# A hybrid recurrent trunk layer in float32: turns of two output tiles in one place, level 0 of an inversion turned by a product, another order of the first loads, shorter last row pieces

## The chip, the cores and the metric

The kernel runs on one core of a Trainium2 chip. Its metric is the device time of one execution in microseconds, the median of three runs. The engines that count here are TensorE (PE in the rows; its weight loads are PEld), VectorE (DVE), ScalarE (ACT), GpSimd (POOL) and the sync engine's queue that issues every DMA (SP). Each engine executes its own instructions in order, and waits between engines are semaphores.

## What is computed

One layer over 592 rows of width 2048: 64 rows of a later-chunk request, 16 learned meta rows and 512 rows of a prompt.

```
h = rmsnorm(x, norm_pre);  P = h @ w_in          # 2048 x 15504
A: mLSTM, 8 heads x 128      B: HGRN2, 4 heads x 128      C: RWKV-7, 8 heads x 64
merged = sum_b sigmoid(gate_b(h)) * (y_b @ w_proj_b)
x' = x + rmsnorm(merged @ w_out, norm_post)      # 576 rows are kept

rwkv_step:
    sa = einsum('bhvk,bhk->bhv', s_state, -kk)
    s_new = s_state * w + sa (kk * a)^T + v k^T
    y = einsum('bhvk,bhk->bhv', s_new, r)
```

The outputs are the rows of x' and the states of the three branches. The RWKV branch is done in chunks of up to 128 rows, for which a unit lower triangular matrix has to be inverted per chunk and head.

## The kernel before

**Products.** Every weight tile is a block of 2048 x 128 float32 values. It comes by DMA to `w_raw` (two slots), ScalarE rounds it to `w_hi` (`split_hi`), VectorE takes the rest into `w_lo` (`split_lo`), and `product(n)` (line 990) multiplies it in 16 blocks by the activations, which are kept in the same way as `act_hi` and `act_lo`. One block is three matmuls (hi by hi, lo by hi, hi by lo) per range of columns. `stages` hangs other TensorE work ahead of a given block, so that it runs inside the stream of matmuls.

**Start.** SP issues the loads in the order of lines 725 to 733: the vectors of weights (`vecs`), rows 0 to 127 of x, the constants (`full`, which holds the identity), the other rows of x, two weight tiles, the masks. For each of five row tiles ScalarE squares the rows (line 1698), GpSimd makes 1/rms of the sums in two small operations (lines 3031, 3033), VectorE scales the rows (line 2166), and TensorE turns them. VectorE's loop stands behind `dve.wait_ge(vecs_here, 16)` at line 2161, ScalarE's behind the same wait at line 1691. The first product needs the fifth row tile.

**RWKV.** There are four rounds, each with two heads. The inversion keeps the inverse of the levels done so far in `DD1` and goes up through levels 0 to 6. Level 0 is made by VectorE in `EE0` (lines 2642 to 2644) from a block unit matrix that GpSimd writes (line 3073). TensorE turns `EE0` by ten transposes (`turn_first`, line 1368, which calls `turn_squares`) ahead of block 19, and ScalarE copies the result to `DD1` in five pieces (`squares_out`, line 1948). Level 1 begins ahead of block 22 (`level_a_d(1)`), and its second half stands ahead of block 24 (`level_d_a_d(1)`, L1322 in rows) and waits for VectorE's step `low1`. Between `inv0` and `low1` VectorE has the token shift of v (`mixed`, lines 2153 to 2156), a `split_lo` and the masking of level 1.

**Output.** The last stage multiplies by w_out in two parts p: columns 0 to 319 and then 320 to 575, 16 tiles each. When a tile is done, ScalarE copies it out of PSUM (`evacuate`, line 2112, into `zt[0]` or `zt[1]`), TensorE turns it into rows (`turn_out`, line 1622; three transposes for p = 0, two for p = 1), ScalarE sums the squares of these rows (`square_rows`, line 2120), and VectorE stores the scaled rows in `YT` (`rows_out`, line 2969). The loops of TensorE take tiles 2i+1 and 2i+2 per round, the loops of ScalarE tiles 2i and 2i+1. ScalarE's order in a round is

```
evacuate(2i); split_hi(2i+2); square_rows(i, 0); evacuate(2i+1); split_hi(2i+3); square_rows(i, 1)
```

and `turn_out(p, i, j)` waits for `evacuate(2i+j)`, `square_rows(i, j)` for `turn_out(p, i, j)`. At the end of a round TensorE waits in `rows_taken` for the squares and rows of `j = 1`.

**End.** After the last tile VectorE finishes row tiles 3 and 4 (`finish`, line 2985) in halves of 1024 columns, and SP stores each half behind the count `rows_done`.

## Time and profile before

| what | us |
|---|---|
| median of three runs | 2223.01 |
| lowest and highest | 2221.34, 2223.16 |
| the profiled execution | 2221.52 |
| its span, first to last instruction | 2219.7 |
| TensorE busy in it | 2186.7 |
| VectorE, ScalarE, GpSimd busy | 1347.9, 788.0, 63.8 |

The rows quoted further down are of the profiled execution. "Busy" says that an engine had an instruction in flight. A row of the timeline gives start, length, engine, source line, operation and tiles; matmuls overlap, so that the cost of one is the distance between two starts and not its length. What stands in brackets is the idle time of the engine before it and what ended it.

### The profile page before, as it was taken

How to read it: one execution, taken by the hardware profiler on the slowest of the kernel's cores; microseconds unless marked ns; L12 is line 12 of the kernel's file. 1: busy time of each engine (PE TensorE's matmuls, PEld its weight loads, DVE VectorE, ACT ScalarE, POOL GpSimd, SP SyncE). 2: the span in 40 equal slices, each digit the busy share in tenths (PEclk: the TensorE clock that was granted, in tenths of full speed). 3: DMA queues.
4: the chain of work that ended last, by engine and by line, in shares of the span. 5: the costliest groups of instructions: out<-in, count | busy, mean ns of one | idle time of the engine just before them, and what ended most of it. 6: DMA issues, size and time to landing. Idle time of an engine off the chain costs nothing.

```text
span 2219.7 us, 44655 instructions
## 1 busy us (share of the span) xinstructions
PE 2186.7 (99%) x18901; PEld 2151.0 (97%) x18901; DVE 1347.9 (61%) x2105; ACT 788.0 (36%) x1209; POOL 63.8 (3%) x93
## 2 busy tenths in 40 slices
PE   6999999999999999999999999999999999999997
PEld 5999999999999999999999999999999999999997
DVE  5444444488777777676657484755777755454354
ACT  5321221234333333333334242424333443244443
POOL 0000001000000000000000000000000000000000
PEclk9999999999999999999999999999999999999999
DMA  5422222233333333334112121204111353434465
GB/s 184 134 79 97 84 86 90 76 106 119 121 135 110 120 120 124 126 119 169 59 52 83 42 74 45 88 22 151 67 67 67 112 207 139 163 138 171 151 216 181
DMA packets 67352, 249.33 MB, mean 112 GB/s; under 512 B 9082, under 2 KB 16428, under 8 KB 50612
## 3 DMA queue, kind: packets, MB, share of 16 engines
q1 hardware_dynamic: 67204, 247.14, 32.1%
q8 instruction: 120, 1.97, 0.4%
q14 instruction: 28, 0.23, 0.0%
HBM read 216.92 MB, written 30.19 MB: 111 GB/s over the span
## 4 chain that ended last, share of the span: by engine, by line
PE 98%; DMA 1%; DVE 0%; SPq 0%; ACT 0%; issue 0%; DVEq 0%; POOL 0%; ACTq 0%; POOLq 0%
PE acc L1009 52%; PE acc L1198 16%; PE branch L1198 8%; PE acc L1608 7%; PE branch L1608 2%; PE branch L1297 1%; PE branch L1497 1%; PE branch L1313 1%; PE branch L1322 1%; DMA scratch<-in_x_all 1%; PE acc L1052 1%; PE branch L1287 0%; PE branch L1365 0%; PE branch L1628 0%; PE branch L1144 0%; PE branch L1137 0%
## 5 line engine op out<-in xcount | busy, mean ns | idle before, releaser
L1009 PE MATMUL acc<-act_hi,w_hi 128*128 128x320 f32 (+3 forms) x2848 | 869.0, 305 | 0.0
L1009 PE MATMUL acc<-act_lo,w_hi 128*128 128x320 f32 (+3 forms) x2848 | 845.4, 297 | 0.0
L1009 PE MATMUL acc<-act_hi,w_lo 128*128 128x320 f32 (+3 forms) x2848 | 845.4, 297 | 0.0
L1009 PEld LDWEIGHTS acc<-act_hi,w_hi 128*128 128x128 f32 x2848 | 537.3, 189 | 11.0 <-issue 5.0
L1009 PEld LDWEIGHTS acc<-act_lo,w_hi 128*128 128x128 f32 x2848 | 537.2, 189 | 0.7
L1009 PEld LDWEIGHTS acc<-act_hi,w_lo 128*128 128x128 f32 x2848 | 537.0, 189 | 0.0
L2149 DVE TENSOR_TENSOR w_lo<-w_raw,w_hi 128x2048 fp32r<-128x2048 f32 x119 | 272.5, 2290 | 228.1 <-ACT w_hi L1666 225.6
L1666 ACT ACTIVATE w_hi<-w_raw 128x2048 fp32r<-128x2048 f32 x120 | 229.8, 1915 | 132.9 <-PE branch L1608 125.7
L1198 PE MATMUL acc<-corner_terms,w_hi 128*128 128x288 f32 x768 | 154.5, 296 | 0.0
L1198 PE MATMUL acc<-act_hi,w_hi 128*128 128x288 f32 x512 | 151.6, 296 | 0.0
L1198 PE MATMUL acc<-act_lo,w_hi 128*128 128x288 f32 x512 | 151.4, 296 | 0.0
L1198 PE MATMUL acc<-act_hi,w_lo 128*128 128x288 f32 x512 | 151.0, 295 | 0.0
L1198 PEld LDWEIGHTS acc<-corner_terms,w_hi 128*128 128x128 f32 x768 | 123.1, 188 | 0.0
L1816 ACT ACTIVATE w_hi<-w_raw 128x1024 fp32r<-128x1024 f32 x72 | 76.2, 1060 | 126.3 <-PE acc L1198 82.9
L1608 PE MATMUL acc<-act_lo,w_hi 128*128 128x288 f32 x384 | 113.4, 295 | 0.0
L1816 ACT ACTIVATE w_hi<-scratch 128x1024 fp32r<-128x1024 f32 x72 | 76.2, 1058 | 104.4 <-PE acc L1198 55.8
L1608 PE MATMUL acc<-act_hi,w_hi 128*128 128x288 f32 x384 | 113.2, 295 | 0.0
L1608 PE MATMUL acc<-act_hi,w_lo 128*128 128x288 f32 x384 | 113.1, 294 | 0.0
L1198 PE MATMUL acc<-corner_terms,w_lo 128*128 128x288 f32 x384 | 113.1, 294 | 0.0
L2346 DVE TENSOR_TENSOR w_lo<-w_raw,w_hi 128x1024 fp32r<-128x1024 f32 x72 | 87.8, 1219 | 36.7 <-ACT w_hi L1816 36.7
L1678 ACT ACTIVATE scratch<-acc 128x64 f32<-128x64 f32 (+1 forms) x38 | 8.3, 219 | 254.5 <-PE acc L1009 254.5
L1198 PEld LDWEIGHTS acc<-act_hi,w_lo 128*128 128x128 f32 x512 | 96.5, 188 | 0.0
(470 smaller groups left out, 3502.9 us busy)
## 6 DMA issues: line engine op xcount, KB each, us to landing
w_raw<-in_w_stream SPq DMA_DIRECT2D x122, 1024.0 KB, 4.8
w_raw<-in_w_stream SPq DMA_DIRECT2D x96, 512.0 KB, 5.9
gate_logits<-gate_out SPq DMA_DIRECT2D x48, 288.0 KB, 2.2
scratch<-gate_logits SPq DMA_DIRECT2D x48, 288.0 KB, 5.2
scratch<-in_x_all SPq DMA_DIRECT2D x9, 512.0 KB, 6.0
branch_rows<-branch_out SPq DMA_DIRECT2D x16, 288.0 KB, 2.2
scratch<-in_x_all SPq DMA_DIRECT2D x3, 1024.0 KB, 10.7
out_y_prompt<-scratch SPq DMA_DIRECT2D x6, 512.0 KB, 3.0
```

Of the source, the lines that this page charges most:

```text
L1009: last = mm(acc[s][:, at:at + hi - lo], a[:, s, w], b[:, k, lo:hi], start=(k == order[0] and a is whi and b is xh), stop=(k == order[-1] a ...
L1052: last = mm(acc[0][:, at:at + hi - lo], a[:, 0, P * k:P * k + P], b[:, k, lo:hi], start=(k == 0 and a is whi and b is xh), stop=(k == KT - ...
L1198: last = mm(bank, a[slot][:, w], b[:, k, :], start=(k == 0 and a is q_hi and b is x[0]), stop=(k == KH - 1 and a is q_lo))
L1297: last = mm(bank[:, P * c:P * c + P], lhs[r, span(c)], rhs[r, span(c)], start=True, stop=True)
L1313: last = mm(bra[to, JOIN_AT + 32 * n:JOIN_AT + 32 * n + 32], AT[r, q, r], first, start=True, stop=True)
L1322: last = mm(bra[r, o:o + 32], d, UU[at_, n, 0:32], start=True, stop=True)
L1497: last = mm(brb[r, o + 64 * c:o + 64 * c + 64], k[:, tok], q[:, tok], start=True, stop=True)
L1608: last = mm(banks3[b][:, at:at + hi - lo], x[:, s, w], y[:, k, lo:hi], start=(k == ks[0] and x is whi and y is xh), stop=(k == ks[-1] and ...
L1666: f(whi[:, s, :], wraw[:, s, :], ACT.Copy).then_inc(hi_done, 1)
L1816: R_["hi"].done(f(q_hi[slot], src, ACT.Copy), name)
L2149: v.tensor_tensor(wlo[:, s, :], wraw[:, s, :], whi[:, s, :].bitcast(F32), ALU.subtract).then_inc(lo_done, 1)
L2346: return R.done(v.tensor_tensor(out, a, b, op), step)
```

## The change

There are five edits.

1. The loads are issued as x rows 0 to 127, x rows 128 to 255, `full`, the rest of x, `vecs`, the two weight tiles, the masks. ScalarE's wait for `vecs` moves behind its squares. VectorE's wait for `vecs` stays where it was, ahead of its first scaling (line 2167 now).
2. `full` gets two columns of zeros ahead of the identity, so that `next_row`, the identity moved by one column, can be read from it.
3. RWKV level 0: `turn_first` waits for the step `yk1` and issues one matmul of 320 columns. VectorE subtracts its result from a second block unit matrix, which GpSimd writes into `DD1`. The copy of one block of `EE0`, the ten transposes and ScalarE's five copies are gone. Level 1 waits for VectorE's `turned_inv0`.
4. Output stage: both turns of a round stand ahead of block 3 of product 2i+2; product 2i+1 has none. This holds for seven rounds of each part. ScalarE's and VectorE's order is as before.
5. Row tiles 3 and 4 are finished and stored in pieces of 512, 512, 1024 and 1024, 512, 512 columns.

```diff
-    full = {"ident": np.eye(P), "blocks": s // 64 == t // 64}
+    full = {"lead": np.zeros((P, 2)), "ident": np.eye(P), "blocks": s // 64 == t // 64}
...
+        next_row = full[:, CONST_AT["ident"][0] - 1:CONST_AT["ident"][1] - 1]
...
+        LAST_PIECES = [(3, (0, D // 4)), (3, (D // 4, D // 2)), (3, (D // 2, D)), (4, (0, D // 2)), (4, (D // 2, D // 4 * 3)), (4, (D // 4 * 3, D))]
...
-            sp.dma_start(vecs[:, :], vecs_in).then_inc(vecs_here, 16)
             for t in range(5):
                 for a, b, src in given(t, ROWS[t]):
                     sp.dma_start(xt[a:b, t, :], src).then_inc(x_here[t], 16)
-                if t == 0:
+                if t == 1:
                     sp.dma_start(full[:, :], full_in).then_inc(consts_here, 16)
+            sp.dma_start(vecs[:, :], vecs_in).then_inc(vecs_here, 16)
...
-            for m in range(4):
+            for m in range(len(LAST_PIECES)):
                 sp.wait_ge(rows_done, 4 + m)
-                rows_out(3 + m // 2, m % 2)
+                last_rows_out(m)
...
                     if lv == 1:
-                        pe.wait_ge(*at.after(i, "t0"))
+                        pe.wait_ge(*vt.after(i, "turned_inv0"))
...
                 def turn_first():
-                    pe.wait_ge(*vt.after(i, "inv0"))
-                    turn_squares(EE0, 0)
+                    pe.wait_ge(*vt.after(i, "yk1"))
+                    pt.done(mm(brb[:, 0:320], next_row, UU[:, :, 0:32], start=True, stop=True), "turned0")
...
-                    product(OUT_N + 1, {3: [lambda: turn_out(0, 0, 0)], 4: [lambda: pe.wait_ge(lo_done, OUT_N + 2)]},
-                            unevacuated=KT, cols=cols[0], in_pieces=True)
-                    product(OUT_N + 2, {3: [lambda: turn_out(0, 0, 1)]}, unevacuated=KT, cols=cols[0])
+                    product(OUT_N + 1, {4: [lambda: pe.wait_ge(lo_done, OUT_N + 2)]}, unevacuated=KT, cols=cols[0], in_pieces=True)
+                    product(OUT_N + 2, {3: [lambda: turn_out(0, 0, 0), lambda: turn_out(0, 0, 1)]}, unevacuated=KT, cols=cols[0])
                     rows_taken(0, 0)
                 with looped(pe, 1 - p, top) as i:
-                    product(Num(OUT_N + KT * p, 2, i, 1), {3: [lambda: turn_out(p, i, 0)]}, unevacuated=KT, cols=cols[p])
-                    product(Num(OUT_N + KT * p, 2, i, 2), {3: [lambda: turn_out(p, i, 1)]}, unevacuated=KT, cols=cols[p])
+                    product(Num(OUT_N + KT * p, 2, i, 1), unevacuated=KT, cols=cols[p])
+                    product(Num(OUT_N + KT * p, 2, i, 2), {3: [lambda: turn_out(p, i, 0), lambda: turn_out(p, i, 1)]}, unevacuated=KT, cols=cols[p])
                     rows_taken(p, i)
...
-            act.wait_ge(vecs_here, 16)
             act.wait_ge(*S0["setup_pool"].after(0, "zeros"))
...
+            act.wait_ge(vecs_here, 16)
             act.wait_ge(w_here[0], 16)
...
-                act.wait_ge(*G.after(i, "turned0"))
-                squares_out(lambda r, qs: DD1[r, qs, :], 0)
...
-                tt(EE0[:, 0:10, 1::2], EE0[:, 0:10, 1::2], UU[:, :, 0:32], ALU.subtract, "inv0_part")
-                own("inv0_part")
-                V.done(v.tensor_copy(EE0[64:128, 10, :], EE0[64:128, 0, :]), "inv0")
+                tt(EE0[:, 0:10, 1::2], EE0[:, 0:10, 1::2], UU[:, :, 0:32], ALU.subtract, "inv0")
+                dve.wait_ge(*Q.after(i, "turned_unit_blocks"))
+                dve.wait_ge(*G.after(i, "turned0"))
+                tt(DD1[:, 0:10, 0::2], DD1[:, 0:10, 0::2], brb[:, 0:320].rearrange("p (q n) -> p q n", q=10), ALU.subtract, "turned_inv0")
...
+                Q.done(g.tensor_tensor(DD1[:, 0:10, :], each, each, ALU.mult), "turned_unit_blocks")
                 Q.done(g.memset(DDT[:, :, :], 0.0), "square_zeros")
```

How the instructions stand at the places that matter is shown in three pairs. The first is SP's queue at the start, before.

```order
L725 DMA vecs<-in_vecs_in 128x109
L728 DMA scratch<-in_x_all 64x2048 x2
L730 DMA full<-in_full_in 128x256
L728 DMA scratch<-in_x_all 128x2048 x3
L728 DMA scratch<-in_x_all 64x2048
L728 DMA scratch<-in_x_all 16x2048
L732 DMA w_raw<-in_w_stream 128x2048 x2
```

And the same place of the changed kernel.

```order
L729 DMA scratch<-in_x_all 64x2048 x2
L729 DMA scratch<-in_x_all 128x2048
L731 DMA full<-in_full_in 128x258
L729 DMA scratch<-in_x_all 128x2048 x2
L729 DMA scratch<-in_x_all 64x2048
L729 DMA scratch<-in_x_all 16x2048
L732 DMA vecs<-in_vecs_in 128x109
L734 DMA w_raw<-in_w_stream 128x2048 x2
```

The vectors moved behind all rows of x. VectorE's first row of the changed kernel is still `L2172 TENSOR_SCALAR` with a wait for `vectors_loaded`.

The second place is VectorE at level 0 of the RWKV inversion, before. The first row writes `EE0`, the copy makes its eleventh block, and the row of 593 columns is the first step of v's token shift.

```order
L2522 TENSOR_TENSOR scratch<-scratch 128x320 [waits rwkv_vector]
L2519 REGISTER_ALU
L2644 COPY scratch<-scratch 64x64 [waits rwkv_vector]
L2153 TENSOR_TENSOR scratch<-scratch 128x593 [waits tile_evacuated]
L2154 REGISTER_ALU
L2155 SCALAR_TENSOR_TENSOR scratch<-scratch,head_scalars 128x64 [waits rwkv_vector]
L2156 SCALAR_TENSOR_TENSOR scratch<-scratch,head_scalars 128x528
```

The same place of the changed kernel.

```order
L2528 TENSOR_TENSOR scratch<-scratch 128x320 [waits rwkv_vector]
L2649 REGISTER_ALU
L2650 REGISTER_ALU [waits rwkv_pool]
L2528 TENSOR_TENSOR scratch<-scratch,branch 128x320 [waits rwkv_tensor]
L2159 TENSOR_TENSOR scratch<-scratch 128x593 [waits tile_evacuated]
L2160 REGISTER_ALU
L2161 SCALAR_TENSOR_TENSOR scratch<-scratch,head_scalars 128x64 [waits rwkv_vector]
L2162 SCALAR_TENSOR_TENSOR scratch<-scratch,head_scalars 128x528
```

The copy is replaced by an operation that waits for GpSimd and for TensorE's new matmul, and everything behind it on VectorE stands behind that wait.

The third place is TensorE in the loop of the output stage for p = 0, before. The rows with gate_out are one `turn_out`.

```order
L1009 MATMUL acc<-act_lo,w_hi 128x320
L1009 MATMUL acc<-act_hi,w_lo 128x320
L1625 REGISTER_ALU
L1628 MATMUL branch<-full,gate_out 128x128 [waits tile_evacuated]
L1628 MATMUL branch<-full,gate_out 128x128
L1628 MATMUL branch<-full,gate_out 64x128
L1009 MATMUL acc<-act_hi,w_hi 128x320
L1009 MATMUL acc<-act_lo,w_hi 128x320
```

The same place of the changed kernel, in product 2i+2.

```order
L1018 MATMUL acc<-act_hi,w_lo 128x320
L1637 MATMUL branch<-full,gate_out 128x128 [waits tile_evacuated]
L1637 MATMUL branch<-full,gate_out 128x128
L1637 MATMUL branch<-full,gate_out 64x128
L1634 REGISTER_ALU
L1637 MATMUL branch<-full,gate_out 128x128 [waits tile_evacuated]
L1637 MATMUL branch<-full,gate_out 128x128
L1637 MATMUL branch<-full,gate_out 64x128
L1018 MATMUL acc<-act_hi,w_hi 128x320
```

The second turn, with its own wait for an evacuation, now follows the first without a matmul between them. ScalarE, which serves both waits, has in the changed kernel the order that it had:

```order
L2126 ISA [waits out_tensor]
L2126 ACTIVATE branch_out,mlstm_scalars<-branch 128x128
L2126 ISA
L2126 ACTIVATE branch_out,mlstm_scalars<-branch 128x128
L2126 ISA
L2126 ACTIVATE branch_out,mlstm_scalars<-branch 64x128
L2116 REGISTER_ALU
L2118 ACTIVATE gate_out<-acc 128x320 [waits tile_product_done]
L1674 ACTIVATE w_hi<-w_raw 128x2048 [waits tile_product_done,weights_loaded1]
```

The three squares wait for the first turn (`out_tensor`), and the evacuation of the odd tile (L2118) stands behind them.

## Rows read from the trace of the kernel before

**Rows 1.** The page's busy times: engine, us, share of the span, instructions.

```profile
PE 2186.7 (99%) x18901; PEld 2151.0 (97%) x18901; DVE 1347.9 (61%) x2105; ACT 788.0 (36%) x1209; POOL 63.8 (3%) x93
```

**Rows 2.** Timeline of TensorE, output stage p = 0: start, length, operation.

```profile
2004.52 0.31 PE L1009 MATMUL acc<-act_hi,w_lo 128*128 128x320 f32 x1
2004.67 0.49 PE L1628 MATMUL branch<-full,gate_out 128*128 128x128 f32 x3
...
2005.15 0.31 PE L1009 MATMUL acc<-act_lo,w_hi 128*128 128x320 f32 x1
```

**Rows 3.** Timeline of TensorE, output stage p = 1.

```profile
2185.24 0.29 PE L1009 MATMUL acc<-act_hi,w_lo 128*128 128x256 f32 x1
...
2185.36 0.38 PE L1628 MATMUL branch<-full,gate_out 128*128 128x128 f32 x2
...
2185.70 0.28 PE L1009 MATMUL acc<-act_lo,w_hi 128*128 128x256 f32 x1
```

**Rows 4.** Timeline of ScalarE and VectorE, output stage p = 0.

```profile
2003.52 0.44 ACT L2112 ACTIVATE gate_out<-acc 128x320 f32<-128x320 f32 x1 [2.27 <-PE acc L1009]
...
2005.65 0.27 ACT L2120 ACTIVATE branch_out<-branch 128x128 f32<-128x128 f32 x1
...
2006.31 0.20 ACT L2120 ACTIVATION_READ_ACCUMULATOR branch_out<-branch  x1
...
2005.80 2.29 DVE L2149 TENSOR_TENSOR w_lo<-w_raw,w_hi 128x2048 fp32r<-128x2048 f32 x1 [0.93 <-ACT w_hi L1666]
2008.00 0.42 DVE L2969 TENSOR_TENSOR scratch<-branch,scratch 128x256 f32 x1
```

**Rows 5.** Timeline of the end, all engines.

```profile
2208.06 0.38 ACT L2112 ACTIVATE gate_out<-acc 128x256 f32<-128x256 f32 x1 [3.96 <-PE acc L1009]
...
2208.50 0.44 PE L1628 MATMUL branch<-full,gate_out 128*128 128x128 f32 x2 [0.47 <-ACT gate_out L2112]
...
2209.03 0.28 ACT L2120 ACTIVATE branch_out<-branch 128x128 f32<-128x128 f32 x1 [0.59 <-PE branch L1628]
...
2211.03 4.87 DVE L2985 SCALAR_TENSOR_TENSOR scratch<-scratch,small 128x1024 f32<-128x1024 f32 x4 [0.82 <-DVE scratch L2969]
...
2212.34 3.92 SPq L953 DMA_DIRECT2D out_y_prompt<-scratch  x4
```

**Rows 6.** Timeline of the start, ScalarE and VectorE.

```profile
12.33 1.29 DVE L2166 TENSOR_SCALAR scratch<-scratch,small 128x2048 f32<-128x2048 f32 x1 [12.33 <-POOL small L3033]
...
21.29 1.91 ACT L1698 ACTIVATE scratch<-scratch 80x2048 f32<-80x2048 f32 x1 [1.64 <-DMA scratch<-in_x_all]
...
23.51 0.63 ACT L1700 ACTIVATE w_hi<-w_raw 128x512 fp32r<-128x512 f32 x1 [0.22 <-DMA w_raw<-in_w_stream]
...
24.23 0.42 DVE L2166 TENSOR_SCALAR scratch<-scratch,small 80x384 f32<-80x384 f32 x1 [2.36 <-POOL small L3033]
```

**Rows 7.** Timeline of TensorE, first RWKV round, and one float32 product.

```profile
1060.70 0.66 PE L1266 MATMUL branch<-scratch,full 128*128 128x296 f32 x2
...
1090.02 0.28 PE L1009 MATMUL acc<-act_hi,w_lo 128*128 128x272 f32 x1
1090.23 1.31 PE L1365 MATMUL branch<-full,scratch 128*128 128x128 f32 x10
1091.30 0.40 PE L1009 MATMUL acc<-act_hi,w_hi 128*128 128x320 f32 x1
...
1097.03 1.36 PE L1322 MATMUL branch<-scratch 64*64 64x32 f32 x40
```

**Rows 8.** Timeline of VectorE and GpSimd, first RWKV round.

```profile
1090.21 1.96 DVE L2153 TENSOR_TENSOR scratch<-scratch 128x593 f32<-128x593 f32 x1
...
1095.33 0.49 DVE L2522 TENSOR_TENSOR scratch<-branch,masks 128x320 f32<-128x320 f32 x1
...
1087.76 1.26 POOL L3073 TENSOR_TENSOR scratch<-masks 128x640 f32<-128x640 bf16 x1 [46.96 <-PE branch L1297]
...
1090.08 1.45 POOL L3076 TENSOR_TENSOR corner_terms<-scratch,corner_terms 128x592 fp32r<-128x592 f32 x1
```

19 lines of the change are left out of this document (13 added, 6 removed).

## The prediction

> **What bounds the kernel now.** I read the page's busy times first: TensorE is busy for 2186.7 us of the 2219.7 us span [rows 1]. The rest is the start, where it waits for the first rows of x, and the end, where the last rows are normalised and stored. So an edit is worth what it does to TensorE's own stream, to the time at which that stream starts, or to what follows its last matmul. Busy time saved on VectorE, ScalarE or GpSimd is worth nothing unless TensorE waits for it. Then I read the timeline at the four places the edits touch: both parts of the output stage [rows 2, 3, 4], the end [rows 5], the start [rows 6] and level 0 of the RWKV inversion [rows 7, 8]. At each I ask two things: how long TensorE's own work takes there, and how early the others are with what it waits for next.
>
> The sum is made against the profiled execution, 2221.5 us, which is 1.5 us below the median of 2223.0.
>
> **The output turns.** A place with three transposes costs TensorE 0.33 us: from 2004.52 to 2005.15 are 0.63 us, of which two steps of 0.15 us are matmuls [rows 2]. A place with two costs 0.22 us: 0.46 us less two steps of 0.12 us [rows 3]. The third transpose is therefore worth 0.11 us and two are worth 0.22 us, so no fixed price of a place is left that sharing one could save. I take 0.0 us for it, and 0.1 us a round (twice the 0.05 us that reading two starts can miss) as the most it could give.
>
> What the edit adds is a wait. In the shared place the second turn waits for the evacuation of tile 2i+1. On ScalarE that evacuation stands behind `square_rows(i, 0)`, which waits for the first turn, which is issued just ahead of it in the same place. Before the change the first turn had been done a whole product earlier, and ScalarE was free when tile 2i+1 ended. Now TensorE's queue stands still while ScalarE does the squares and the evacuation, and nothing else is in that queue to fill the time. The price, counted from the start of the first turn, for p = 0:
>
> - the three transposes end after 0.49 us [rows 2];
> - ScalarE starts 0.08 us after the end of a turn (2208.50 + 0.45 to 2209.03) [rows 5], at 0.57;
> - three squares with their sums take 0.86 us (2005.65 to 2006.31 + 0.20) [rows 4], to 1.43;
> - the evacuation of 320 columns takes 0.44 us [rows 4], to 1.87;
> - TensorE starts 0.06 us after the end of an evacuation (2208.06 + 0.38 to 2208.50) [rows 5], at 1.93;
> - the second turn and the way back into the matmuls cost 0.33 us, to 2.26.
>
> Two separate places cost 0.66 us, so a round costs 1.60 us more. For p = 1 the terms are 0.38, 0.08, two squares in 0.61 (0.86 less one step of 0.25), 0.38, 0.06 and 0.22, together 1.73 us against 0.44: 1.29 us more. There are seven such rounds in each part: 7 x 1.60 + 7 x 1.29 = **+20.2 us**. From below the wait can't be shorter than the evacuation and the squares without the two hand-overs (1.46 and 1.15 us, 18 us in all). From above each round may lose another 0.4 us to register work and to starting ScalarE cold: 26 us.
>
> Is anything late next? The odd tile's weights are rounded behind that evacuation. Before, the low part began 2.28 us after the evacuation's start, took 2.29 us, and the row operation after it ended at 2008.42, which is 4.90 us after [rows 4]. TensorE, for p = 1, needs 0.38 + 0.06 + 0.22 us and 13 blocks of three matmuls at 0.12 us [rows 3], 4.68 us, so it comes to the end of the product 5.34 us after the evacuation's start. That leaves some 0.4 us. For p = 0 the product is longer and the margin over 1 us. Only in the first round of p = 1, where VectorE also finishes 128 rows of the first part, do I expect it to be used up; 0.2 us is inside the rounding of the sum.
>
> **The start.** ScalarE and SP no longer wait for the vectors, but VectorE's first scaling does, and the vectors are now queued behind all of x. Before, the scaling of the first row tile began at 12.33 us, and the first 384 columns of the fifth began at 24.23 us [rows 6]; only the fifth was on the path. The last rows of x landed at 21.3 us (ScalarE's square at 21.29 had waited for them) and the first weight tile at 23.5 us [rows 6]. The vectors are queued between the two. The bytes ahead of the vectors' end are the same as those ahead of x's end before, so I take 21.3 us; 23.5 us is the other end. From then VectorE has four scalings of up to 1.29 us [rows 6] to do that were all done before; at 1.25 us each the fifth starts at 26.3 us in place of 24.23: +2.1 us. GpSimd's two small operations for the fifth tile, which lay in the 1.03 us between the square's end (23.20) and 24.23, now fall between VectorE's scalings; I add 0.3 us for that. **+2.4 us**. Everything on TensorE behind it moves by that much, since the fifth tile's turns release the first product. The ends are: nothing at all (the small load overtakes x; even 0.4 us earlier, as x is issued earlier) and +4.3 us (the vectors land with the weights). Issuing x first gains nothing while VectorE waits. The later `full` is hidden, as the first turn is later still.
>
> The Trainium skill (SBUF — State Buffer, Who interferes with whom) says that VectorE's `tensor_scalar` can run in a mode that locks a port shared with GpSimd, and that whoever starts first blocks the other for the whole instruction. By that rule each of GpSimd's two operations could wait for the end of a scaling and hold the next one up by its own length; the 0.3 us would then be up to 0.75 us. No row of the kernel before has the two beside each other at the start.
>
> **Level 0 of the RWKV inversion.** TensorE came to block 19 at about 1090.15 us (0.13 after 1090.02) and was back in its matmuls at 1091.30: 1.15 us, of which ten transposes are 1.07 us [rows 7]. The new matmul has 320 float32 columns; two of 296 columns took 0.66 us, the second of them ending 0.41 us after its start, so one step is 0.25 us [rows 7], and 320 columns are 0.27 us. TensorE saves 1.15 - 0.27 = 0.88 us a round. It is back only if VectorE keeps up, and VectorE now waits for this matmul. The matmul ends at 1090.15 + 0.43, VectorE's subtraction from PSUM takes 0.49 us, as the operation of that size at 1095.33 did [rows 8], and the token shift of v starts at about 1091.14 in place of 1090.21 [rows 8]: 0.93 us later. Before, `low1` was done at 95.33 + 0.49 = 1095.82, and TensorE asked for it at 1097.03 [rows 7, 8], so the reserve was 1.2 us. Now `low1` comes at 1096.75 and TensorE, 0.88 us earlier, asks at 1096.15. It waits 0.6 us, and 0.23 us a round are left. Four rounds: **-0.8 us** (I round down what is left, since GpSimd is busy longer too). ScalarE's five copies were never waited for.
>
> The step of 593 columns at 1090.21 took 1.96 us, though the operation of 320 columns took 0.49 us, and GpSimd's operation of 592 columns lay over it, from 1090.08 to 1091.53 [rows 8]. So about 1.1 us of it were a wait for GpSimd. GpSimd gets one more operation of 1.26 us [rows 8], so its operation of 592 columns starts at about 1091.3, just behind VectorE's step. If VectorE gets through first and isn't held up later, it wins 1.1 us, TensorE doesn't wait, and the gain is 4 x 0.88 = 3.5 us. If it is held up in the next step for all of 1.45 us, 0.25 us more are lost and the gain is 0. I take the middle, the same hold-up as before.
>
> The same section of the Trainium skill says that a VectorE operation with two SBUF inputs contends with a GpSimd operation that reads SBUF, and that the order of issue decides who blocks. The row agrees with the first half. By the second VectorE's step would pass, GpSimd would take the port when it ends, and VectorE's next step would be held up in its place; the sum of this part would then be 0 to -0.8 us.
>
> **The end.** VectorE finishes the last rows in four pieces in 4.87 us, SP issues their stores from 2212.34 on, and the span ends at 2219.7 [rows 5]. With a first piece of half the size the first store starts some 0.55 us earlier, and with a last store of half the size less is left behind the last piece, whose data come about 0.25 us later, as there are two instructions more. **-0.4 us**, between 0 and -0.6.
>
> Sum: 2221.5 + 20.2 + 2.4 - 0.8 - 0.4 = 2242.9 us, and with the 1.5 us of the median **2244.4 us**.
>
> **The rivals.**
> - *The turns don't stop TensorE.* If tile 2i+1 were evacuated ahead of the squares of tile 2i, the shared place would cost nothing. Then 2221.5 + 2.4 - 0.8 - 0.4 + 1.5 = 2224.2 us, no change; with the most that sharing could give, 1.4 us, 2222.8. The mechanism decides the sign as soon as the wait is below 0.3 us a round. Against it stands ScalarE's order, which the change leaves as it was. 3 in 100.
> - *The weights become late in part 1.* With a margin of 0.4 us, a hand-over that is slower by more than that makes the product behind each round wait too: 7 x 0.5 = +3.5 us, 2247.9 us. 10 in 100.
> - *VectorE passes GpSimd in the RWKV part.* -2.7 us, 2241.7 us. 10 in 100.
> - *The vectors land early*, because small loads overtake large ones: -2.6 us, 2241.8 us. 6 in 100.
> - *TensorE's clock falls in the stops.* The rows show steps of 0.15 and 0.12 us at either end of the stage [rows 2, 3], the higher of the two levels, and the stage has no such stop now. If one tile in four ran at half that pace, 8 of 32 tiles would add 48 steps of 0.12 to 0.15 us each, 5.8 to 7.2 us: some 50 us, 2295 us. 4 in 100.
>
> **How the numbers follow.** The forecast has what is left, 67 in 100, with a range of its own of 2240 to 2249 us from the ends of the output term (-2, +4 of its +6) and of the start (-2, +2). The range that should hold the time 8 times in 10 is 2238 to 2251 us: it takes in the RWKV, vector and weight rivals. A measurement of this kernel can tell about 0.2%, 4.4 us, from no change. Faster than that has 1 in 100, within it 3 in 100, slower 96 in 100.
>
> **What would show it.** In the profile of the changed kernel TensorE should have 14 waits at the turns, released by ScalarE's evacuation, of about 1.4 us (p = 0: second turn 1.9 us after the first) and 1.1 us (p = 1), and two tiles should take 1.6 and 1.3 us more than two tiles of before. VectorE's first scaling should start at 21 to 22 us, waiting for the vectors, and the first product at 28 to 29 us instead of 26. In the RWKV rounds one matmul of 320 columns should stand where ten transposes stood, and TensorE should wait for `low1` at block 24. Wrong it would be if those 14 waits are missing, if they are a multiple of this length, or if the matmuls of the output stage have steps other than 0.15 and 0.12 us.

## The result

| kernel | median us | lowest, highest | ratio to the kernel before, 95% interval | profiled execution, its span |
|---|---|---|---|---|
| before | 2222.31 | 2221.34, 2223.16 | | 2221.52, 2219.7 |
| changed | 2249.56 | 2247.88, 2250.57 | 1.0125 [1.0112, 1.0137] | 2249.42, 2247.6 |

The changed kernel is 27.3 us slower by the medians and 27.9 us by the spans. The forecast was 2244.4 us, its range 2238 to 2251. The direction came as forecast, and so did the first part of the output stage. The second part of it, the RWKV rounds, a stretch that the change doesn't touch and the end all came out slower than forecast, the start a little faster.

The page's busy times of the changed kernel, which answer to [rows 1]. TensorE is busy for 3.7 us more in a span that is 27.9 us longer; for the other 24 us it stood still. The mean granted clock is 0.998 in both profiles.

```profile
PE 2190.4 (97%) x18869; PEld 2149.9 (96%) x18869; DVE 1353.0 (60%) x2107; ACT 782.7 (35%) x1189; POOL 71.0 (3%) x97
```

Where the time went is read best from an engine that works seldom. GpSimd's operations stand at fixed places of the program, so the distance between the same two of them in both traces is the length of a stage. (The last of the four RWKV rounds is counted up to the first HGRN operation, so that row of the table takes in the start of HGRN.) The timeline of GpSimd, kernel before:

```profile
46.39 0.20 POOL L3038 COPY scratch<-vecs 128x1 f32<-128x1 f32 x1
...
1586.66 0.48 POOL L3085 TENSOR_SCALAR small<-o_sums 128x5 f32<-128x5 f32 x1 [64.81 <-ACT scratch L2060]
...
2119.06 0.19 POOL L3092 TENSOR_SCALAR small<-small 128x3 f32<-128x3 f32 x1 [343.13 <-DVE small L2981]
...
2209.97 0.19 POOL L3092 TENSOR_SCALAR small<-small 128x2 f32<-128x2 f32 x1 [89.79 <-DVE small L3004]
```

The same operations in the changed kernel, with the first of the RWKV rounds, which is in [rows 8] for the kernel before:

```profile
48.11 0.20 POOL L3046 COPY scratch<-vecs 128x1 f32<-128x1 f32 x1
...
1091.07 1.26 POOL L3081 TENSOR_TENSOR scratch<-masks 128x640 f32<-128x640 bf16 x1 [46.91 <-PE branch L1306]
...
1591.02 0.47 POOL L3094 TENSOR_SCALAR small<-o_sums 128x5 f32<-128x5 f32 x1 [65.37 <-ACT scratch L2066]
...
2134.80 0.20 POOL L3101 TENSOR_SCALAR small<-small 128x3 f32<-128x3 f32 x1 [354.44 <-DVE small L2988]
...
2237.44 0.20 POOL L3101 TENSOR_SCALAR small<-small 128x2 f32<-128x2 f32 x1 [101.51 <-DVE small L3011]
```

The starts that the table needs beside these are 446.61 and 448.51 us (the last mLSTM operation) and 1774.76 and 1779.19 us (the last HGRN operation). The differences, beside the terms of the forecast:

| stage, between which starts | before | changed | difference | forecast |
|---|---|---|---|---|
| start, 0 to the copy | 46.39 | 48.11 | +1.7 | +2.4 |
| to the last mLSTM operation | 400.22 | 400.40 | +0.2 | 0 |
| from there to the first RWKV round | 641.15 | 642.56 | +1.4 | 0 |
| the RWKV rounds, to the first HGRN operation | 498.90 | 499.95 | +1.1 | -0.8 |
| HGRN | 188.10 | 188.17 | +0.1 | 0 |
| output, first part (p = 0) | 344.30 | 355.61 | +11.3 | +11.2 |
| output, second part (p = 1) | 90.91 | 102.64 | +11.7 | +9.0 |
| end, to the end of the span | 9.73 | 10.16 | +0.4 | -0.4 |
| sum | 2219.7 | 2247.6 | +27.9 | +21.4 |

**The output places.** TensorE's waits in the output stage of the changed kernel (engine, line, what it waited for: us in total, times, longest). The kernel before had only the last of the 15 at L1637, of 0.47 us [rows 5].

```profile
PE branch L1637 <- ACT gate_out L2118: 17.7, 15, 1.4
PE acc L1018 <- ACT gate_out L2118: 0.6, 1, 0.6
```

One place of each part in TensorE's timeline, to set beside [rows 2, 3]; the first two rows are of p = 0, the others of p = 1:

```profile
2016.17 0.49 PE L1637 MATMUL branch<-full,gate_out 128*128 128x128 f32 x3
2018.04 0.55 PE L1637 MATMUL branch<-full,gate_out 128*128 128x128 f32 x3 [1.38 <-ACT gate_out L2118]
...
2209.70 0.38 PE L1637 MATMUL branch<-full,gate_out 128*128 128x128 f32 x2
2211.16 0.44 PE L1637 MATMUL branch<-full,gate_out 128*128 128x128 f32 x2 [1.08 <-ACT gate_out L2118]
...
2211.56 0.28 PE L1018 MATMUL acc<-act_lo,w_hi 128*128 128x256 f32 x1
```

And ScalarE between the two turns at p = 0, as [rows 4] for the kernel before. The evacuation stands behind the six operations of the squares; it starts at 2017.56, and the second turn follows 0.05 us after its end.

```profile
2016.79 0.28 ACT L2126 ACTIVATE branch_out<-branch 128x128 f32<-128x128 f32 x1 [6.59 <-PE branch L1637]
...
2017.56 0.43 ACT L2118 ACTIVATE gate_out<-acc 128x320 f32<-128x320 f32 x1
```

**The end of a round at p = 1.** Here is the part of the output that the forecast missed. TensorE's matmuls follow each other every 0.12 us, but at the loop's turn 0.33 us lie between two starts, and 0.22 us between the next two: 0.3 us are lost, though the profile lists no wait there. VectorE's row operation, for which TensorE waits there in `rows_taken`, ended at 2215.15 + 0.42 = 2215.57, 0.69 us ahead of the matmul that begins the next round. TensorE's timeline, then VectorE's:

```profile
2215.93 0.28 PE L1018 MATMUL acc<-act_hi,w_lo 128*128 128x256 f32 x1
2216.26 0.38 PE L1018 MATMUL acc<-act_hi,w_hi 128*128 128x256 f32 x1
...
2215.15 0.42 DVE L2976 TENSOR_TENSOR scratch<-branch,scratch 128x256 f32 x1
```

### The profile page after: what moved, and what is told of

Same layout as the page of the kernel before. It is cut to its first block and busy times, and to the rows that moved or that the text cites. A ratio compares the mean times of both kernels' runs of the same rounds, so it can differ in the third digit from the quotient of the medians.

```text
span 2247.6 us, 44567 instructions
## 1 busy us (share of the span) xinstructions
PE 2190.4 (97%) x18869; PEld 2149.9 (96%) x18869; DVE 1353.0 (60%) x2107; ACT 782.7 (35%) x1189; POOL 71.0 (3%) x97
```

## The experiments

Every kernel was profiled once and timed in three or five rounds beside the kernel before. The changes of stage that follow are read from GpSimd's operations, as above. The spans of two profiles (ScalarE's order and VectorE's wait moved) hold one stop of TensorE at the end of the output rounds of p = 0 that no engine had caused ("issue", 2.5 and 1.7 us). That of the turns apart has two rounds of p = 1 in which the weights landed late (TensorE waited 0.7 and 0.6 us, and the part is 1.8 us longer than in the kernel before). The changed kernel's own profile has neither, and the medians serve for the totals there.

**The changed kernel again.** It gives the repeat: 2249.42 us (2248.22 to 2249.78), ratio 1.0124 [1.0107, 1.0141]. Against the kernel before its start came out at +2.2 us (first profile +1.7), the RWKV rounds at +0.7 (+1.1), every other stage within 0.4 us of the first profile. The 1.4 us of the stretch that the change doesn't touch are there again, so they are no chance. The start is what varies most: over the nine profiles with the changed start it is +0.7 to +2.4 us, since the last rows of x land anywhere from 20.1 to 21.3 us.

> The changed kernel once more, so that the others of this call can be compared with it on one chip. Expected about 27 us over the kernel before (2249.6 against 2222.3 us so far). In its trace the stretch from 450 to 1050 us, which the change doesn't touch, took 1.4 us longer than in the kernel before. If that was chance, it goes elsewhere or away in this run; if it comes from the change (another place of the code in memory, another phase of the engines), it is there again.

**The turns apart.** The output edit undone, everything else kept:

```
-product(Num(OUT_N + KT * p, 2, i, 1), unevacuated=KT, cols=cols[p])
-product(Num(OUT_N + KT * p, 2, i, 2), {3: [lambda: turn_out(p, i, 0), lambda: turn_out(p, i, 1)]}, ...)
+product(Num(OUT_N + KT * p, 2, i, 1), {3: [lambda: turn_out(p, i, 0)]}, ...)
+product(Num(OUT_N + KT * p, 2, i, 2), {3: [lambda: turn_out(p, i, 1)]}, ...)
```

> The changed kernel with the turns of the output stage in two places as before; the other four edits stay. Theory: the output edit is worth the 23.0 us by which that stage grew in the trace, so this is about 4 us over the kernel before: +1.8 at the start, 0 to +0.3 in the RWKV rounds, up to +2 of the untouched stretches, -0.4 at the end. Rival: the start costs more than its 1.8 us in the trace, through VectorE being late; then over 6 us.

Measured: 2225.78 us (2225.49 to 2229.67), ratio 1.0022 [1.0012, 1.0031]. Of the 27.3 us 23.8 are gone, which is the output stage's 23.0 us and what the theory said. The other edits together cost 3.5 us against the first median of the kernel before (2222.31), and 4.2 us against the one taken beside this run (2221.55), where the forecast had them at +1.2.

**ScalarE's order.** The turns stay in one place, but ScalarE evacuates and splits both tiles before it squares either:

```
 for j in range(2):
     evacuate(p, n, j)
     split_hi(Num(OUT_N + KT * p, 2, i, j + 2))
+for j in range(2):
     if j: act.wait_ge(...)
     square_rows(p, i, j)
```

> The changed kernel, but in each round of the output stage ScalarE evacuates both tiles and splits both weight tiles, and only then sums the squares of both. Theory: the shared place costs TensorE time only because the evacuation of the odd tile stands behind squares that wait for the first turn. Then the 14 waits of 1.1 to 1.4 us at the turns are gone, and so are the 0.3 us at the end of each round of part 1: 23 us less than the changed kernel, about 4 us over the kernel before. Rival: sharing a place itself costs (six or four transposes in a row, a longer break in the stream of matmuls); then most of the waits are gone but a part of the 23 us stays, over 3 us.

Measured: 2234.91 us (2232.97 to 2238.55), ratio 1.0057 [1.0041, 1.0074]. In TensorE's timeline the wait is gone and six transposes stand together, at the same place as above:

```profile
2016.10 0.82 PE L1637 MATMUL branch<-full,gate_out 128*128 128x128 f32 x6
...
2016.90 0.31 PE L1018 MATMUL acc<-act_lo,w_hi 128*128 128x320 f32 x1
```

From 2016.10 to 2016.90 are 0.80 us, of which one step of 0.15 is a matmul: 0.65 us, twice the 0.33 us of a place with three. So a shared place saves nothing even where nobody waits, as the forecast took it. Two tiles of p = 0 take 14.68 to 14.73 us here (14.69 before, 16.27 to 16.33 in the changed kernel). The wait at the place is thus caused by ScalarE's order and by nothing else. But the total missed the theory, which had some 4 us over the kernel before: the median is 13.4 us over the one taken beside it, and even the lowest of its four times is 11.4 us over. The rival's cause, a price of the shared place itself, isn't it, by the 0.65 us. What costs is the round's end, since the squares and rows of both tiles now come later. The two largest of TensorE's waits in the output stage:

```profile
PE acc L1018 <- issue: 3.1, 3, 2.5
PE acc L1018 <- DVE scratch L2977: 2.7, 1, 2.7
```

The 2.7 us stand at the end of the first round of p = 1, where VectorE also has the finish of the first part's rows (2.34 us each); that round takes 15.96 us from one shared place to the next. The later ones take 12.4 to 12.6 us, against 11.8, and at each turn of the loop among them TensorE starts 0.69 to 0.75 us after the end of the row operation.

**The second turn later.** In the loops, the turn of the odd tile at block 8 of the product, that of the even tile left at block 3:

```
-{3: [lambda: turn_out(p, i, 0), lambda: turn_out(p, i, 1)]}
+{3: [lambda: turn_out(p, i, 0)], 8: [lambda: turn_out(p, i, 1)]}
```

> The changed kernel with the turns of the odd tile five steps of the product later (at block 8 of it instead of block 3), those of the even tile left where they are. Theory (ScalarE makes evacuation, split, squares of the even tile and only then the evacuation and split of the odd one, so TensorE at block 3 is 1.4 us early for them, 15 times): the waits of 1.4 us at the turns are gone, and two places of three transposes cost what they did in the kernel before, since these don't overlap with anything. But the round's end is untouched: the rows of the odd tile still come late, and TensorE waits there 0.8 us a round in the first part and 1.2 to 1.5 in the second, so most of the loss moves and stays: 2236 to 2246. Rival (the place was the whole loss, and the slack at the round's end takes up a turn that is five steps later): the loss of 23 us in the output stage goes down to under 6, 2227 to 2232.

Measured: 2246.95 us (2245.65 to 2248.04), ratio 1.0113 [1.0097, 1.0128], 1 us above what the theory allowed, and far from the rival's 2227 to 2232. The waits at the turns go down by 15.9 us, and there are waits of 13.0 us at the round's end (0.6 in the changed kernel). TensorE's waits in the output stage, and the last one in its timeline, with VectorE's operation that it waited for:

```profile
PE acc L1018 <- DVE scratch L2976: 9.8, 7, 1.9
PE acc L1018 <- ACT gate_out L2118: 3.2, 5, 0.7
PE branch L1637 <- ACT gate_out L2118: 1.8, 2, 1.4
...
2213.23 0.38 PE L1018 MATMUL acc<-act_hi,w_hi 128*128 128x256 f32 x1 [1.38 <-DVE scratch L2976]
...
2212.12 0.41 DVE L2976 TENSOR_TENSOR scratch<-branch,scratch 128x256 f32 x1
```

The row operation ended at 2212.53 and TensorE's next matmul started at 2213.23, 0.70 us later. In the changed kernel the same distance is 2216.26 - 2215.57 = 0.69 us. These are no single cases: at the six turns of the loop in p = 1 the distance is 0.69 to 0.76 us in the changed kernel and 0.69 to 0.71 us in this run. At a turn of the loop TensorE's queue thus took 0.7 us from the end of what it waited for to its matmul, where a wait inside the stream (the second turn above) took 0.05 us. At the end of the last round, where the loop is left, this run has 0.38 us. That the distances agree, with long waits and with none listed, is what shows that the time lost at the round's end is a wait for the row operation.

**VectorE's wait for vecs moved too.** The changed kernel with

```
+            dve.wait_ge(vecs_here, 16)      # behind the scalings, ahead of the first use of vecs
-            dve.wait_ge(vecs_here, 16)      # ahead of the first scaling
```

> The changed kernel with one more thing moved: VectorE waits for vecs behind its scalings of x instead of ahead of them, as ScalarE already does. Theory (the start lost its gain to VectorE, whose first scaling stood behind vecs, at 20.94 us, though its rows of x had long landed, and whose scaling then shared the time with GpSimd's small operations): VectorE's first scaling starts when the square of tile 0 is done, some 5 us earlier; the first product, 1.8 us later than in the kernel before, comes about 0.6 us earlier than in it, so the whole is 2.4 us faster than the changed kernel, at about 2247. Rival (the first product waits for its weights, or for the split on GpSimd, whichever way x comes): the first product stays within 0.5 us of 27.84 us, and the whole within 0.5 us of 2249.4.

Measured: 2247.05 us (2246.77 to 2249.21), ratio 1.0112 [1.0097, 1.0128]: 2.4 us below the changed kernel, as the theory said. The start in the changed kernel, VectorE and GpSimd:

```profile
20.94 5.36 DVE L2172 TENSOR_SCALAR scratch<-scratch,small 128x2048 f32<-128x2048 f32 x5 [20.94 <-DMA vecs<-in_vecs_in]
...
22.74 0.73 POOL L3039 TENSOR_SCALAR small<-small 80x1 f32<-80x1 f32 x1 [2.69 <-ACT scratch L1705]
23.55 2.30 POOL L3041 TENSOR_TENSOR small<-small,minus_half 80x1 f32<-80x1 f32 x1
```

And with VectorE's wait moved:

```profile
11.80 1.29 DVE L2171 TENSOR_SCALAR scratch<-scratch,small 128x2048 f32<-128x2048 f32 x1 [11.80 <-POOL small L3041]
...
23.81 0.42 DVE L2171 TENSOR_SCALAR scratch<-scratch,small 80x384 f32<-80x384 f32 x1 [2.61 <-POOL small L3041]
...
22.96 0.19 POOL L3039 TENSOR_SCALAR small<-small 80x1 f32<-80x1 f32 x1 [3.08 <-ACT scratch L1705]
23.23 0.55 POOL L3041 TENSOR_TENSOR small<-small,minus_half 80x1 f32<-80x1 f32 x1
```

The fifth tile's scaling starts at 23.81 us; it was 24.23 in the kernel before [rows 6]. The first product starts at 25.61 us, 0.4 us earlier than before, where the changed kernel has it at 27.84. Over all profiles it starts at 26.0 and 26.6 us with the old order, at 25.0 to 25.8 us (three profiles) with the new order and no engine waiting for the vectors, and at 27.3 to 28.4 us (nine) where VectorE waits. So the new order of the loads is worth a little at the first product, but only if no engine waits for the load that was put last; how much it is worth can't be told from the scatter. GpSimd's two operations for the fifth tile took 0.73 and 2.30 us beside VectorE's scalings and 0.19 and 0.55 us without them. The Trainium skill (SBUF — State Buffer, Who interferes with whom) says that VectorE's `tensor_scalar` can take the port that it shares with GpSimd for the whole instruction and block the other; the rows agree: GpSimd's operation ended at 25.85 us, 0.04 us after VectorE's fourth scaling, and the fifth started at 25.88. Most of the 2.30 us were hidden beside the scalings, which followed each other every 1.20 us; some 0.16 us came on top.

**Level 0 as before.** The RWKV edit undone, everything else kept (`turn_first` again with ten transposes, ScalarE's five copies, VectorE's small copy, GpSimd without the second block).

> The changed kernel with level 0 of the RWKV inversion as before: EE0 turned by ten transposes, five copies on ScalarE, no second block matrix on GpSimd. Theory: the product takes two passes of 0.28 us and TensorE then waits 0.7 us a round for VectorE, which GpSimd holds up, so the edit is worth nothing: within 1 us of the changed kernel. Rival: the wait is a loss of its own; then this is 2 to 3 us faster than the changed kernel. Second rival: the four waits of 0.7 us hide a gain of 0.6 us a round against the ten transposes; then this is 2 us slower.

Measured: 2248.66 us (2247.01 to 2249.01), ratio 1.012 [1.0103, 1.0137], and the medians alone don't tell it from the changed kernel. The stage does: the RWKV rounds take 0.3 us less than in the kernel before here (as they do with two columns alone, below), and 0.5 to 1.1 us more with the edit. The edit costs about 1 us where the forecast had it win 0.8. The waits in this stage of the changed kernel, of which there are none with level 0 as before:

```profile
PE branch L1331 <- DVE scratch L2528: 3.0, 4, 0.7
PE branch L1506 <- DVE scratch L2836: 0.5, 1, 0.5
```

The second one stands behind the RWKV rounds, in the first round of HGRN at 1563 us, and it is in every kernel with the edit (0.2 to 0.5 us) and in none without it. Ahead of it VectorE stood still for 1.5 to 1.8 us with nothing that the profile shows to wait for; without the edit that stop takes 0.8 to 1.3 us and comes one operation later. Why is open. The wait is about a third of what the edit costs.

**GpSimd's operation first.** The changed kernel with `bonus_lo` moved ahead of GpSimd's wait for the product yk_:

```
+pool.wait_ge(*Sc.after(i, "bonus_hi"))
+Q.done(g.tensor_tensor(bon_lo_r, bon, bon_hi_r.bitcast(F32), ALU.subtract), "bonus_lo")
 pool.wait_ge(*G.after(i, "yk_"))
 ... unit_blocks, turned_unit_blocks, square_zeros ...
-pool.wait_ge(*Sc.after(i, "bonus_hi"))
-Q.done(g.tensor_tensor(bon_lo_r, bon, bon_hi_r.bitcast(F32), ALU.subtract), "bonus_lo")
```

> The changed kernel with one operation of GpSimd moved in each round of the RWKV inversion: the low part of bonus (1.47 us, at 1094.60 us in round 1), which stood behind the two unit blocks and the zeros, goes ahead of the wait for the product yk_, since its inputs are there 10 us earlier. Theory (TensorE waits 0.74 us a round for low1 because VectorE is late, and VectorE is late because its operation of 593 columns at 1094.61 us takes 2.10 us beside this one of GpSimd, where alone it would take about 0.85): that operation of VectorE takes under 1 us, the 4 waits of together 3.0 us are gone, and the whole is 2.5 to 3.5 us faster than the changed kernel, 2246.4. Rival (VectorE is late because of the product with its 320 columns and the addition of turned_inv0, which now stand in its way): the waits shrink by less than a third and the whole stays within 1 us of 2249.4.

Measured: 2245.85 us (2244.74 to 2246.74), ratio 1.0108 [1.0093, 1.0124]: 3.6 us below the changed kernel, and no wait for `low1` is left. The RWKV round in the changed kernel, VectorE, GpSimd and TensorE (the rows that answer to [rows 7, 8]):

```profile
1092.49 1.40 DVE L2528 TENSOR_TENSOR scratch<-scratch 128x320 f32<-128x320 f32 x1
...
1094.61 2.10 DVE L2159 TENSOR_TENSOR scratch<-scratch 128x593 f32<-128x593 f32 x1
...
1092.28 1.26 POOL L3082 TENSOR_TENSOR scratch<-masks 128x640 f32<-128x640 bf16 x1
...
1094.60 1.47 POOL L3085 TENSOR_TENSOR corner_terms<-scratch,corner_terms 128x592 fp32r<-128x592 f32 x1
...
1093.45 0.72 PE L1379 MATMUL branch<-scratch,full 128*128 128x320 f32 x2
...
1094.15 0.30 PE L1018 MATMUL acc<-act_lo,w_hi 128*128 128x320 f32 x1
```

VectorE's timeline with GpSimd's operation first:

```profile
1091.41 1.39 DVE L2528 TENSOR_TENSOR scratch<-scratch 128x320 f32<-128x320 f32 x1
...
1093.53 0.77 DVE L2159 TENSOR_TENSOR scratch<-scratch 128x593 f32<-128x593 f32 x1
```

The operation of 593 columns takes 0.77 us alone and 2.10 us beside GpSimd's. The other hold-up is still there: VectorE's subtraction of 320 columns takes 1.39 us beside GpSimd's second block, against 0.48 us in the kernel before:

```profile
1089.19 0.48 DVE L2522 TENSOR_TENSOR scratch<-scratch 128x320 f32<-128x320 f32 x1
```

This agrees with the same section of the Trainium skill, by which a VectorE operation with two inputs in SBUF contends with a GpSimd operation that reads it. By its rule that the order of issue decides who blocks, the forecast saw VectorE's step of 593 columns pass. That case didn't come up: GpSimd's operation started at 1094.60 us and VectorE's at 1094.61, and VectorE's ended 0.64 us after GpSimd's, as it had in the kernel before, where GpSimd's was 0.12 us ahead [rows 8]. With 0.01 us between them the pair neither bears the rule out nor speaks against it.

TensorE's product is two instructions of 128 x 320, for one call in the program. From 1093.45 to 1094.15 are 0.70 us, less one step of 0.15: 0.55 us. The ten transposes before took 1090.15 to 1091.30 and a longer first step behind them, 1.23 us counted in the same way up to the second full step. So the product saves 0.68 us a round, 2.7 in four. The RWKV rounds with GpSimd's operation first take 496.3 us, 2.6 us less than in the kernel before and 2.3 us less than with level 0 as before; the wait of 0.4 us in the first HGRN round, still there, makes up the rest of the 2.7.

**Two columns alone.** The kernel before with nothing but

```
-    full = {"ident": np.eye(P), "blocks": s // 64 == t // 64}
+    full = {"lead": np.zeros((P, 2)), "ident": np.eye(P), "blocks": s // 64 == t // 64}
```

> The kernel before with nothing changed but 2 columns of zeros ahead of the identity in the tile of constants, which no instruction reads. Theory (the shift of 8 bytes of all that lies behind that tile slows TensorE's products by a per cent): the stretch from 447 to 1088 us is 1.4 us longer than in the kernel before, the means of the products of 384 columns go from 294 to 297 ns, and the whole is 1.4 to 2.5 us slower, 2224. Rival (the shift costs nothing): all within 0.3 us of the kernel before.

Measured: 2223.15 us (2221.62 to 2225.06), ratio 1.0005 [0.9996, 1.0014]. The total is 1.2 us over the median beside it (2221.99), a little less than the theory's 1.4 to 2.5, and alone would not tell it; the stage does: 1.4 us longer between the last mLSTM operation and the first RWKV round (642.52 us), as in the changed kernel (642.56); the other stages within 0.3.

**Sixteen columns.** The changed kernel with `np.zeros((P, 16))` in that line, which shifts every tile behind `full` by 64 bytes and not by 8.

> The changed kernel with 16 columns of zeros ahead of the identity instead of 2, so that every tile of SBUF that is laid out behind it is shifted by 64 bytes and not by 8. Theory (the 1.4 us by which the stretch from 447 to 1088 us is longer than in the kernel before, though no instruction of it was changed, are TensorE's products whose moving operand lies at another place: 294 to 297 ns for the 384 columns of w_lo): that stretch is as long as in the kernel before, to 0.3 us, and the whole is 1.4 to 2.5 us faster than the changed kernel. Rival (the stretch is longer for another reason, such as where the loads of the start left the queues, or the instructions' own place): it stays 1.4 us longer, and the time stays.

Measured: 2246.22 us (2245.38 to 2248.35), ratio 1.0111 [1.0096, 1.0127], 3.2 us below the changed kernel. The stretch takes 639.38 us: 3.2 us less than with 2 columns and 1.8 us less than in the kernel before. The theory had the stretch equal to the kernel before, and the total 1.4 to 2.5 us below the changed kernel, and was wrong in both. The matmuls whose moving operand (the one that is streamed past the weights) is `corner_terms`, a tile laid out behind `full` (duration min/median/max in ns), in the kernel before, with the w_hi and w_lo weights:

```profile
L1198 PE MATMUL acc<-corner_terms,w_hi x768: 292/296/299, 508.5 to 1028.4; 128*128 128x288 f32 x192
L1198 PE MATMUL acc<-corner_terms,w_lo x384: 290/295/296, 508.7 to 1028.5; 128*128 128x288 f32 x192
```

The kernel before with 2 columns:

```profile
L1198 PE MATMUL acc<-corner_terms,w_lo x384: 293/297/300, 509.0 to 1030.3; 128*128 128x288 f32 x192
```

The changed kernel with 16 columns:

```profile
L1207 PE MATMUL acc<-corner_terms,w_hi x768: 290/294/298, 510.3 to 1028.6; 128*128 128x288 f32 x192
```

These durations overlap, so the sum of the steps from start to start is the better measure. In the stretch the steps behind the 576 matmuls with w_lo add up to 76.35 us in the kernel before, 77.74 with 2 columns and 76.28 with 16. Those behind the 1152 matmuls with w_hi add up to 153.84, 153.72 and 152.18 us. So the 8 bytes cost 1.4 us with w_lo alone, and the 64 bytes gained 1.7 us with w_hi alone: 2.4 ns a matmul in the one case, 1.4 in the other. The matmuls whose moving operand is `act_hi` or `act_lo`, which lie ahead of `full`, change by under 0.2 us in all. So the place of the moving operand is worth one or two per cent of a matmul, in either direction. Why one place is better than another stays open: three places are too few for a rule.

**The end as before.** The changed kernel with the last two tiles finished and stored in four halves:

```
-for u, (a, b) in LAST_PIECES:
-    if u == t:
-        finish(t, a, b)
+for h in range(2):
+    finish(t, h * D // 2, h * D // 2 + D // 2)
```

and SP's loop over the stores with it.

> The changed kernel with the last two tiles finished and stored in four halves, as in the kernel before, and not in six pieces. Theory (three small pieces more cost VectorE 0.26 us and SyncE two issues, and the last store, though half as large, landed 3.1 us after its issue as the large one did, so the smaller pieces bring nothing): from the last GpSimd operation on the output to the end 9.7 us and not 10.16, the whole 0.4 us faster than the changed kernel, which five rounds hardly tell from nothing; the profile's end does. Rival (the late landing in the changed kernel was an accident of that run, and the smaller last store does come 0.4 us earlier): the end is 0.4 us longer with the halves.

Measured: 2249.38 us (2248.36 to 2250.02), ratio 1.0124 [1.0108, 1.0139]; the total shows nothing. The end does, read from GpSimd's last operation but one: it takes 9.70 us here (2236.80 to 2246.5), 9.73 in the kernel before, 10.16 in the changed one. The changed kernel's end, VectorE and SP, which answers to [rows 5]:

```profile
2238.51 5.13 DVE L2992 SCALAR_TENSOR_TENSOR scratch<-scratch,small 128x512 f32<-128x512 f32 x6 [0.82 <-DVE scratch L2976]
...
2239.29 4.78 SPq L951 DMA_DIRECT2D out_y_prompt<-scratch  x6
```

With four halves:

```profile
2237.86 4.87 DVE L2991 SCALAR_TENSOR_TENSOR scratch<-scratch,small 128x1024 f32<-128x1024 f32 x4 [0.82 <-DVE scratch L2975]
...
2239.17 3.92 SPq L961 DMA_DIRECT2D out_y_prompt<-scratch  x4
```

The first store is issued 0.78 us after VectorE's start with the pieces and 1.31 us after it with the halves: 0.53 us earlier. But from that first issue to the end are 8.32 us with the pieces and 7.37 us with the halves (and 7.37 us in the kernel before), 0.95 us more. The queue of stores shows why. One row of each trace, the us from 2241 to 2242, pieces first (busy times of PE, PEld, DVE, ACT, POOL, then the clock, the busy share of the DMA engines and their GB/s):

```profile
2241.00:2242.00 1.00, 0.00 (x0) 0.00 (x0) 1.00 (x2) 0.00 (x0) 0.00 (x0) 0.50 0.59 223
...
2241.00:2242.00 1.00, 0.00 (x0) 0.00 (x0) 1.00 (x2) 0.00 (x0) 0.00 (x0) 0.50 1.02 410
```

With the halves the DMA engines are full, at 401 to 410 GB/s, from 2240 us until shortly before the last store lands. With the pieces they do the two small stores and then run partly empty, because the third piece is a large one and its store is issued only 1.20 us after the second's; behind that they are full as well, at 361 to 406 GB/s. So the end follows the bytes that are still to be stored and not the size of the last store: the earlier start is lost again in the gap, and 0.4 us with it. This is read from the two traces; no run tried other sizes.

**What is left as a gain.** Two kernels put together what the runs left. Both have the turns apart and the end as before, the rows of x first with VectorE's wait moved, and 16 columns. One has level 0 as before, the other the product with GpSimd's `bonus_lo` first.

> Only what the runs so far left as a gain: rows of x ahead of vecs with VectorE's wait for vecs moved as well, 16 columns ahead of the identity, everything else (turns of the output, level 0, last stores) as in the kernel before. Theory (the first two parts are independent of the rest): start within 0.3 us of the kernel before, the stretch from 447 to 1088 us 1.8 us shorter, the rest the same: 2220, 1.5 to 2.5 us faster than the kernel before. Rival (the place of the tiles changes something later, as the stretch of HGRN does by 1 us in the run with 16 columns): within 0.5 us of the kernel before.

> The last kernel with the RWKV edit put back in (level 0 by a product) and GpSimd's bonus_lo moved ahead of it. Theory (the RWKV edit saves TensorE 0.55 to 0.88 us a round and lost it only to the wait for low1): about 2.3 us faster than the last kernel, 2218. Rival (the product of 320 columns as two instructions and its place ahead of the weights cost what the four turns did): within 0.5 us of the last kernel.

| kernel | median us | lowest, highest | ratio, 95% interval | span |
|---|---|---|---|---|
| level 0 as before | 2219.05 | 2218.01, 2220.18 | 0.9986 [0.9977, 0.9995] | 2216.8 |
| level 0 by the product | 2217.96 | 2216.59, 2220.26 | 0.9984 [0.9975, 0.9993] | 2214.8 |

Both are faster than the kernel before, by 3.3 and 4.4 us of the medians (2222.32 us over the 21 runs of it by then). The first is 0.8 us better than its theory's upper end (2.5 us). In its trace 1.8 us are the stretch from mLSTM to RWKV and 1.1 us the start. The second has 0.9 us at the start, but the run in which only VectorE's wait was moved had none at the same operation, and the same start code of the changed kernel varies by 1.7 us there; so what the order of the loads is worth stays between 0 and 1 us. That nothing would be won, the first one's rival, falls. Of the product, the trace shows 2.2 us in the RWKV rounds, as its theory had it (2.3 us), and the medians 1.1 us, halfway to its rival; by their intervals the two kernels can't be told apart.

## Why the prediction was right, and where it was not

**Output, p = 0: +11.2 forecast, +11.3 measured.** Each step of the chain is in the trace. The second turn starts 1.87 us after the first (forecast 1.93), and two tiles take 16.27 to 16.33 us where they took 14.69: 1.6 us a round, forecast 1.60. The working was right because the wait could be built from rows of the same operations on the same engines. That sharing the place saves nothing was right too (0.65 us for six transposes).

**Output, p = 1: +9.0 forecast, +11.7 measured.** The place itself is as priced: 2211.16 - 2209.70 = 1.46 us between the turns (forecast 1.51), and from 2209.58, the last step ahead of it, to 2211.56 are 1.98 us, of which two steps of 0.12 are matmuls: 1.74 us where two places had cost 0.44, so 1.3 us more, the term. The step that failed is "That leaves some 0.4 us". It set the end of the row operation (4.90 us) beside the end of TensorE's product (5.34 us) without a hand-over between them. At the loop's turn that hand-over is 0.7 us, so the rounds are late by 0.7 - 0.4 = 0.3 us; the trace has 0.34 to 0.40 in each round behind the first (13.41 to 13.47 us where 11.78 and the 1.29 are 13.07). The first round, where VectorE finishes rows of the first part and TensorE has a listed wait of 0.59 us, takes 13.95 us and loses 0.9. Together that is the 2.7 us. The rival of late weights described this, at 0.5 us a round and with the wrong thing late: it is the rows of the odd tile, not its weights.

**Start: +2.4 forecast, +1.7 measured, +0.7 to +2.4 in nine profiles.** VectorE's first scaling started at 20.94 us (forecast 21.3) and waited for the vectors; the first product came at 27.84, 1.8 us later than before. The mechanism was right. Each step of it was priced a little high: the vectors by 0.4 us, four scalings at 1.20 us and not 1.25 by 0.2 us, and of the 0.3 us for GpSimd only 0.16 were spent, though its operations stretched from 0.74 to 3.03 us together.

**RWKV: -0.8 forecast, +1.1 measured, +0.5 to +1.1 in the eight profiles with the edit as it stands.** Two terms were mis-sized. "One step is 0.25 us, and 320 columns are 0.27 us" took one matmul where there are two instructions, 0.55 us: the saving is 0.68 us a round, not 0.88. And "I take the middle, the same hold-up as before" overlooked that GpSimd's new block lies beside VectorE's subtraction that makes `inv0`: 1.40 us against 0.48. From the masking of yk to that of level 1 VectorE needed 7.61 us before (1087.72 to 1095.33) and 8.80 us now (1091.02 to 1099.82), 1.2 us more, forecast 0.93. TensorE waits 0.74 us a round, forecast 0.6, which is more than the 0.68 saved: four rounds lose 0.2 us where 0.9 were to be won. (The forecast's own 0.88 less 0.6 is 0.28 us and not the 0.23 it went on with, which its rounding hid.) The wait of 0.5 us in the first HGRN round was in no term, the two columns alone made these rounds 0.3 us shorter, and a further 0.7 us of this profile (0.3 to 0.5 in the others) is not accounted for. The mechanism, a wait for `low1` that eats the saving, was right, and the run with GpSimd's operation first shows how the gain is got out.

**End: -0.4 forecast, +0.4 measured.** The first store did start 0.53 us earlier, forecast 0.55. The step that failed is "with a last store of half the size less is left behind the last piece". It took each store by itself, where the DMA engines are full from the first store on. What is left behind the last piece is the queue of stores, and the pieces left a gap in that queue: 8.32 us from the first issue to the end where there had been 7.37.

**The untouched stretch: 0 forecast, +1.4 measured.** The forecast priced `full` as a load and never as a tile with neighbours. The run with the two columns alone shows it.

**The rivals.** That the turns don't stop TensorE, that the vectors land early and that VectorE passes GpSimd are ruled out by the rows above. That TensorE's clock falls in the stops is too: the matmuls of the output stage kept their steps of 0.15 and 0.12 us, and the mean granted clock is 0.998 as before.

By the spans the sum was 21.4 us and 27.9 were measured. The 6.5 us between them are +2.7 (output, p = 1), +1.9 (RWKV), +1.4 (the stretch), +0.8 (end), -0.7 (start) and 0.4 us of small ones. The medians differ by less, 5.2 us, since the kernel before came out 0.7 us below the 2223.0 us that the forecast stood on, and the two medians lie 27.3 us apart. The range of 2238 to 2251 us held the time because the output term, which is four fifths of the loss, was bounded from rows; but the bound of +6 us on it was the size of all that was missed, and 3.8 of the 6.5 us lay elsewhere. That the misses fitted into it is luck, and the narrower range of 2240 to 2249 us for the forecast without rivals was missed by 0.6 us.

## What to carry to other kernels

Before two steps of different age are put in one place of an in-order queue, write down the order in which the other engine serves them: a wait behind a step that this very place releases is paid in full, every round. When a margin is worked out, put the hand-over into it, and take it from a row at the same kind of place, since at a loop's turn it was over ten times that inside the stream here. A load that is put last is only cheap when every engine's wait for it has been moved, and a few columns more in a tile move all the tiles behind it. And a store cut smaller brings nothing where the stores already wait for each other.
